# Softmax of the mix stage: exponentials taken by ScalarE from the score banks, probabilities scaled in four pieces

## What is computed

```python
scores = einsum('bcqhgd,bckhd->bchgqk', qc, kb) * HEAD_DIM ** -0.5      # 128 keys a query
scores = where(valid, scores, finfo(float32).min)
probs = softmax(concatenate([scores, sink], axis=-1), axis=-1)[..., :WINDOW]
out = einsum('bchgqk,bckhd->bcqhgd', probs, vb)
mix = concatenate([out, conv], axis=-1) @ w_o
h = layer_norm(ALPHA * h + mix)
```

## Time and profile before

| what | value |
|---|---|
| median of 3 runs | 2282.29 us (2281.48 to 2282.68) |
| span of the profiled execution, first to last instruction | 2280.0 us |
| TensorE busy (matmul) | 2111.2 us, 93% |
| VectorE busy | 1169.0 us, 51% |
| ScalarE busy | 632.4 us, 28% |
| GpSimd busy | 481.3 us, 21% |
| mean granted clock of TensorE | 0.968 of full speed |

### The profile page before, as it was taken

The page is one execution under the profiler, slowest core; times in us unless marked ns, Lnnn a source line. Parts: engine busy times, 40 slices in busy tenths (PEclk is TensorE's granted clock), DMA queues, the critical chain, the costliest instruction groups (busy, mean ns, idle before and its releaser), DMA issues. The chain is left out here.

```text
span 2280.0 us, 25840 instructions
## 1 busy us (share of the span) xinstructions
PE 2111.2 (93%) x9568; PEld 1717.9 (75%) x9568; DVE 1169.0 (51%) x1238; ACT 632.4 (28%) x912; POOL 481.3 (21%) x317
## 2 busy tenths in 40 slices
PE   4999995789889599999999999999999799999997
PEld 3788884566666378888888888888887588888886
DVE  8698983688888444434424334334344311144333
ACT  4555552344444232221121121121121300031110
POOL 5488773243443200000000000000000000002333
PEclk9999997799999799999999999999999899999999
DMA  6310125223333242112111111111210622342220
GB/s 236 138 43 35 60 74 163 64 91 108 98 100 103 96 149 74 37 37 74 37 37 58 53 37 41 70 37 37 74 37 35 224 76 87 115 134 86 76 87 37
DMA packets 125599, 185.54 MB, mean 81 GB/s; under 512 B 7361, under 2 KB 90305, under 8 KB 122305
## 3 DMA queue, kind: packets, MB, share of 16 engines
q1 hardware_dynamic: 99616, 149.31, 20.1%
q10 hardware_dynamic: 25952, 35.86, 4.4%
HBM read 117.90 MB, written 67.24 MB: 81 GB/s over the span
## 5 line engine op out<-in xcount | busy, mean ns | idle before, releaser
L1387 PE MATMUL u_mm<-u_hT_hi,u_w_hi 128*128 128x512 f32 x1408 | 549.1, 390 | 15.4 <-DVE u_hT_lo L1355 15.4
L1387 PE MATMUL u_mm<-u_hT_lo,u_w_hi 128*128 128x512 f32 x1408 | 548.8, 390 | 0.0
L1387 PE MATMUL u_mm<-u_hT_hi,u_w_lo 128*128 128x512 f32 x1408 | 548.7, 390 | 0.0
L1501 POOL TENSOR_TENSOR d_total<-d_total,d_g 128x1024 f32 x16 | 38.2, 2387 | 1406.1 <-DVE d_total L1588 1406.1
L1321 DVE TENSOR_SCALAR u_y<-u_z,u_taps,u_bias 128x2048 f32<-128x2048 f32 x43 | 57.9, 1347 | 529.9 <-ACT u_z L1269 529.9
L1387 PEld LDWEIGHTS u_mm<-u_hT_hi,u_w_hi 128*128 128x128 f32 x1408 | 265.0, 188 | 70.6 <-DVE u_hT_lo L1355 15.8
L1269 ACT COPY u_z<-u_mm 128x512 f32<-128x512 f32 x176 | 103.2, 587 | 748.8 <-PE u_mm L1387 748.8
L1387 PEld LDWEIGHTS u_mm<-u_hT_hi,u_w_lo 128*128 128x128 f32 x1408 | 265.1, 188 | 55.2
L1387 PEld LDWEIGHTS u_mm<-u_hT_lo,u_w_hi 128*128 128x128 f32 x1408 | 265.1, 188 | 55.1
L1625 PE MATMUL d_y<-d_wd_hi,d_a_hi 128*128 128x512 f32 x704 | 218.9, 392 | 20.7 <-DVE d_wd_lo L1560 20.5
L1625 PE MATMUL d_y<-d_wd_hi,d_a_lo 128*128 128x512 f32 x704 | 217.8, 390 | 0.0
(11 more groups left out here) (172 smaller groups left out, 2506.9 us busy)
## 6 DMA issues: line engine op xcount, KB each, us to landing
u_w_raw<-w_up SPq DMA_DIRECT2D x44, 512.0 KB, 5.8
d_a_raw<-gated_scr SPq DMA_DIRECT2D x32, 704.0 KB, 5.3
gated_scr<-u_y SPq DMA_DIRECT2D x21, 1024.0 KB, 4.6
d_wd_raw<-w_down SPq DMA_DIRECT2D x22, 512.0 KB, 4.7
a_xs<-x SPq DMA_DIRECT2D x16, 512.0 KB, 4.7
m_h_in<-h_scr SPq DMA_DIRECT2D x16, 512.0 KB, 3.4
h_scr<-m_r ACTq DMA_DIRECT2D x16, 512.0 KB, 4.0
h1T_scr<-m_h1T ACTq DMA_DIRECT2D x16, 512.0 KB, 4.4
```

The source lines that it names most:

```text
L1387: last = nc.tensor.matmul(mm[m][n][:], w[:, m, k, :], h[:, k, bass.ts(n, BLK)], start=(k == 0 and w is w_hi and h is hT_hi), stop=(k == KT ...
L1501: nc.gpsimd.tensor_tensor(tile_of(t), tile_of(t), g_bc[:], ALU.mult).then_inc(scaled_ok, 1)
```

## The change

The fifth part of each row of `prob`, the sink's column, goes, and with it `peak`. `soft_shift` becomes `soft_peak`: VectorE takes the maximum, then the negated peak (`fall`, the smaller of minus the scale times the maximum and minus the sink) and `rest`, sink plus `fall`. The instruction over 128x512 that wrote the shifted scores is gone. ScalarE's `exps` reads the score bank itself, in four instructions for each g of 128x128, with the scale as a constant, `fall` as bias for each partition and the sum over the keys put out to `den`; a fifth one takes the exponential of `rest` (128x4). `soft_norm` adds `rest` to `den`, takes the reciprocal, and multiplies the probabilities in four `tensor_scalar` instructions of 128x128, each with one column of `inv` for its partitions.

Each result gets a semaphore of its own. TensorE's `scores` of the next tile waits for the exponentials (`exp_ok`) instead of the shifted scores. VectorE computes `minus_sink` once at the start of the stage. To have enough semaphores, `phase_project` closes its context, and GpSimd clears its range of semaphores, so that `phase_mix` can use them.

```diff
@@ phase_project
         def sem(name):
-            return ctx.enter_context(nc.semaphore(name))
+            used.append(ctx.enter_context(nc.semaphore(name)))
+            return used[-1]
...
+        ctx.pop_all().close()
+        nums = sorted(s.num for s in used)
+        assert nums == list(range(nums[0], nums[-1] + 1))
+        nc.gpsimd.sem_clear(range(nums[0], nums[-1] + 1))
@@ phase_mix
-        prob = sb("m_prob", [P, NKV, GROUPS, KEYS + 1])
-        top, peak = sb("m_top", [P, NKV, GROUPS]), sb("m_peak", [P, NKV, GROUPS])
+        prob = sb("m_prob", [P, NKV, GROUPS, KEYS])
+        top, fall = sb("m_top", [P, NKV, GROUPS]), sb("m_fall", [P, NKV, GROUPS])
+        minus_sink, rest = sb("m_minus_sink", [P, NKV, GROUPS]), sb("m_rest", [P, NKV, GROUPS])
...
             def exps(n, g):
-                act.wait_ge(shift_ok, NKV * n.t + (g + 1))
-                nc.scalar.activation(prob[:, g, :, :], prob[:, g, :, :], ACT.Exp).then_inc(exp_ok, 1)
+                act.wait_ge(fall_ok, NKV * n.t + (g + 1))
+                after(act, probT_ps, NKV * n.t)
+                for a in range(GROUPS):
+                    nc.scalar.activation(prob[:, g, a, :], score[g][:, a, :], ACT.Exp, bias=fall[:, g, a:a + 1], scale=SCALE,
+                                         accum_out=den[:, g, a:a + 1])
+                act.wait_ge(rest_ok, NKV * n.t + (g + 1))
+                nc.scalar.activation(rest[:, g, :], rest[:, g, :], ACT.Exp).then_inc(exp_ok, 1)
...
+            nc.vector.tensor_scalar(minus_sink[:, :, :], sink[:, :, :], -1.0, None, ALU.mult).then_inc(msink_ok, 1)
+            dve.wait_ge(msink_ok, 1)
...
-            def soft_shift(n, g):
-                dve.wait_ge(score_ps, NKV * n.t + (g + 1))
+            def soft_peak(n, g):
+                at = NKV * n.t + (g + 1)
+                dve.wait_ge(score_ps, at)
...
-                nc.vector.tensor_reduce(top[:, g, :], score[g][:, :, :], AX.X, ALU.max).then_inc(soft_seq, 1)
-                dve.wait_ge(soft_seq, soft_at(n, g, 1))
-                nc.vector.scalar_tensor_tensor(out=peak[:, g, :], in0=top[:, g, :], scalar=SCALE, in1=sink[:, g, :], op0=ALU.mult,
-                                               op1=ALU.max).then_inc(soft_seq, 1)
-                dve.wait_ge(soft_seq, soft_at(n, g, 2))
-                after(dve, probT_ps, NKV * n.t)
-                nc.vector.tensor_tensor(prob[:, g, :, KEYS], sink[:, g, :], peak[:, g, :], ALU.subtract).then_inc(soft_seq, 1)
-                nc.vector.scalar_tensor_tensor(out=prob[:, g, :, 0:KEYS], in0=score[g][:, :, :], scalar=SCALE,
-                                               in1=along(peak[:, g, :], KEYS), op0=ALU.mult, op1=ALU.subtract).then_inc(shift_ok, 1)
+                nc.vector.tensor_reduce(top[:, g, :], score[g][:, :, :], AX.X, ALU.max).then_inc(top_ok, 1)
+                dve.wait_ge(top_ok, at)
+                after(dve, exp_ok, NKV * n.t - 1 + g)
+                nc.vector.scalar_tensor_tensor(out=fall[:, g, :], in0=top[:, g, :], scalar=-SCALE, in1=minus_sink[:, g, :],
+                                               op0=ALU.mult, op1=ALU.min).then_inc(fall_ok, 1)
+                dve.wait_ge(fall_ok, at)
+                after(dve, den_ok, NKV * n.t - 1 + g)
+                nc.vector.tensor_tensor(rest[:, g, :], sink[:, g, :], fall[:, g, :], ALU.add).then_inc(rest_ok, 1)

             def soft_norm(n, g):
-                dve.wait_ge(exp_ok, NKV * n.t + (g + 1))
-                nc.vector.tensor_reduce(den[:, g, :], prob[:, g, :, :], AX.X, ALU.add).then_inc(soft_seq, 1)
...
-                nc.vector.reciprocal(inv[:, g, :], den[:, g, :]).then_inc(soft_seq, 1)
...
-                nc.vector.tensor_tensor(prob[:, g, :, 0:KEYS], prob[:, g, :, 0:KEYS], along(inv[:, g, :], KEYS), ALU.mult).then_inc(prob_ok, 1)
+                at = NKV * n.t + (g + 1)
+                dve.wait_ge(exp_ok, at)
+                nc.vector.tensor_tensor(den[:, g, :], den[:, g, :], rest[:, g, :], ALU.add).then_inc(den_ok, 1)
+                dve.wait_ge(den_ok, at)
+                nc.vector.reciprocal(inv[:, g, :], den[:, g, :]).then_inc(inv_ok, 1)
+                dve.wait_ge(inv_ok, at)
+                for a in range(GROUPS):
+                    v = nc.vector.tensor_scalar(prob[:, g, a, :], prob[:, g, a, :], inv[:, g, a:a + 1], None, ALU.mult)
+                v.then_inc(prob_ok, 1)
...
@@ scores of TensorE
-                after(pe, shift_ok, NKV * n.t)
+                after(pe, exp_ok, NKV * n.t)
```

More of the change, by code:

```diff
@@ L122, in sb @@
             return ctx.enter_context(nc.sbuf_tensor(name, shape, dt))
+        used = []
         def sem(name):
-            return ctx.enter_context(nc.semaphore(name))
+            used.append(ctx.enter_context(nc.semaphore(name)))
+            return used[-1]
         hT_hi = sb("a_hT_hi", [P, KT, SEQ], F32R)
@@ L676, in phase_mix @@
         conv_hi_ok, conv_lo_ok, attn_hi_ok, attn_lo_ok = (sem("m_" + n) for n in ("conv_hi", "conv_lo", "attn_hi", "attn_lo"))
-        vw_ok, shift_ok, exp_ok, prob_ok, probT_ok = (sem("m_" + n) for n in ("vw", "shift", "exp", "prob", "probT"))
+        vw_ok, exp_ok, prob_ok, probT_ok = (sem("m_" + n) for n in ("vw", "exp", "prob", "probT"))
+        msink_ok, top_ok, fall_ok, rest_ok, den_ok, inv_ok = (sem("m_" + n) for n in ("msink", "top_ok", "fall_ok", "rest_ok", "den_ok", "inv_ok"))
         resid_ok, lv_ok, ly_ok, norm_ok, scaled_ok, h1_ok, h1T_ok = (sem("m_" + n) for n in ("resid", "lv", "ly", "norm", "scaled", "h1", "h1T"))
-        soft_seq, cn_seq, ln_seq, z_seq, lact_seq, cact_seq, stats_seen = (sem("m_" + n) for n in ("soft_seq", "cn_seq", "ln_seq", "z_seq", "lact_seq", "cact_seq", "stats_seen"))
+        cn_seq, ln_seq, z_seq, lact_seq, cact_seq, stats_seen = (sem("m_" + n) for n in ("cn_seq", "ln_seq", "z_seq", "lact_seq", "cact_seq", "stats_seen"))
         block = ctx.enter_context(nc.Block())
@@ L978, in row_norm @@
                 assert seq.n == 6
-            def soft_at(n, g, k):
-                return n.t * (NKV * 5) + (3 * g + k)
-            def soft_shift(n, g):
-                dve.wait_ge(score_ps, NKV * n.t + (g + 1))
+            def soft_peak(n, g):
+                at = NKV * n.t + (g + 1)
+                dve.wait_ge(score_ps, at)
                 if isinstance(n.t, int) and n.t == 0:
@@ L994, in soft_shift @@
-                nc.vector.tensor_tensor(prob[:, g, :, KEYS], sink[:, g, :], peak[:, g, :], ALU.subtract).then_inc(soft_seq, 1)
-                nc.vector.scalar_tensor_tensor(out=prob[:, g, :, 0:KEYS], in0=score[g][:, :, :], scalar=SCALE,
-                                               in1=along(peak[:, g, :], KEYS), op0=ALU.mult, op1=ALU.subtract).then_inc(shift_ok, 1)
-            def soft_norm(n, g):
-                dve.wait_ge(exp_ok, NKV * n.t + (g + 1))
-                nc.vector.tensor_reduce(den[:, g, :], prob[:, g, :, :], AX.X, ALU.add).then_inc(soft_seq, 1)
-                dve.wait_ge(soft_seq, n.t * (NKV * 5) + (3 * NKV + 2 * g + 1))
-                nc.vector.reciprocal(inv[:, g, :], den[:, g, :]).then_inc(soft_seq, 1)
-                dve.wait_ge(soft_seq, n.t * (NKV * 5) + (3 * NKV + 2 * g + 2))
-                nc.vector.tensor_tensor(prob[:, g, :, 0:KEYS], prob[:, g, :, 0:KEYS], along(inv[:, g, :], KEYS), ALU.mult).then_inc(prob_ok, 1)
+                nc.vector.tensor_reduce(top[:, g, :], score[g][:, :, :], AX.X, ALU.max).then_inc(top_ok, 1)
@@ L1044, in step @@
                     log_gate(c)
-                soft_shift(n, 0)
+                soft_peak(n, 0)
                 if c is not None:
                     swish(c)
-                soft_shift(n, 1)
+                soft_peak(n, 1)
                 if c is not None:
```

## The result

The changed kernel takes 2296.93 us (median of 4 runs, 2294.34 to 2298.28), the kernel before in the same comparison 2282.07 (4 runs, 2281.48 to 2282.68): a ratio of 1.0063 [1.0049, 1.0077]. It is slower by 14.9 us.

What follows compares the result with a forecast made beforehand. The step was taken as a loop through TensorE and VectorE's softmax chain, held by GpSimd; 20.8 + 7.7 + 0.2 = 28.7 us on a span of 2280.0 gave 2308.7, 2311 as median, range 2297 to 2327.

Steps and rivals of the forecast that it cites:

- The pieces wait for GpSimd: In soft_norm, tensor_scalar pieces stand still until the running GpSimd instruction ends; g = 0 is held, g = 1 runs free.
- The signs that the prediction named: Around 560: first addition about 2.2 us, a g = 0 piece 1.5 to 2.3, g = 1 pieces 0.3, TensorE idle before g = 0.
- steps of 24.7 us: Sign in the mix stage: each full step would last 24.7 us if the forecast was right.
- faster: Rival: pieces with a column operand don't wait for GpSimd, only the additions do; 2260 to 2272 us, chance 0.11.
- no difference: Rival: pieces wait, but those of g = 0 all get through between two GpSimd instructions; 2277 to 2282 us, chance 0.06.
- 13 steps x 1.6 = 20.8: Mix stage: the scaling of g = 1 ends 1.6 us later in each of 13 steps, 20.8 us in all.
- the lower bound of 1.3: Least delay a step, if pieces follow each other without any handing over and GpSimd's last short instruction is short.
- the prediction's clock: Time scale of the profiled step of the kernel before whose softmax starts at 560.11, used for all forecast event times.
- 5 x 1.53 = 7.7: TensorE's clock: all 13 steps become the slow kind, five of them losing 1.53 us each; bounds 0 and 20.
- I put 0, with 1 us either way: First two tiles of the mix: passes saved are worth at most what they take; put at 0, 1 us either way.
- Terms of 0 that held: ScalarE's exponentials ready before VectorE wants them, and GpSimd's semaphore clearing covered before its fills: each put at 0.
- the edges with minus_sink: First and last tiles put at 0; minus_sink at the stage start put at 0.2 us, up to 2.

Runs made afterwards that it cites:

- Experiment 3: The changed kernel without GpSimd's gain and bias instructions of the norm after the mix (two over 128x1024 a step): 2217.92 us, 0.9717 of the kernel before.
- experiment 8: The changed kernel with ScalarE's exponentials left in the score bank in PSUM, where the four scaling pieces read them: 2264.07 us, 0.9925 of the kernel before.
- experiment 1: The kernel before with only the scaling of the probabilities split into four tensor_scalar pieces, nothing of ScalarE's part: 2330.71 us, 1.0213 of the kernel before.
- experiment 2: The changed kernel with the scaling put back into one multiplication for each g, ScalarE's exponentials kept: 2297.77 us, 1.0065 of the kernel before.
- experiment 6: The changed kernel with one scaling multiplication for each g, and softmax and conv norm operands in PSUM so neither waits for GpSimd: 2226.78 us, 0.9761 of before.
- 4: The kernel before with only the softmax reciprocals moved from SBUF to a dead corner of the score bank in PSUM: 2252.11 us, 0.9867 of the kernel before.
- 5: The changed kernel with one scaling multiplication for each g, and reciprocals and the exponential of rest in PSUM: 2235.93 us, 0.9805 of the kernel before.
- 7: The kernel before with reciprocals and conv norm in PSUM and exps(n, 1) ahead of conv_root, nothing of the change: 2234.88 us, 0.9797 of the kernel before.

## Why the prediction was right in its mechanism and wrong in its size

**The pieces wait for GpSimd** (right). The signs that the prediction named are in the rows of the result, but for steps of 24.7 us, which are 23.99: the addition of 2.26 ending with L792, a piece of 2.27 ending 0.09 behind L794, the pieces of g = 1 free, L993 1.09 us earlier from L1002 (3.88 against 4.97), the idle time ahead of g = 0. Experiment 3 takes GpSimd's two instructions away and the loss with them, experiment 8 lets the pieces alone go free and ends faster than before. The rivals "faster" and "no difference" fall by the same rows: a piece that meets L794 does not last 0.3, and the pieces do not all get through between two GpSimd instructions.

The Trainium skill (SBUF — State Buffer, Who interferes with whom) says that tensor_scalar can take the pair of ports, and that tensor_reduce never contends. By that rule, the trace agrees: 2.27 us for a piece, and 0.68 for the sum L1000 of experiment 1 beside a running L783.

**"13 steps x 1.6 = 20.8"** (failed in size). From the first maximum to the second transposes it is 12.85 us, before 11.63: 1.22 more a step, 15.9 in all. That is below even the lower bound of 1.3. Laid over the prediction's clock (5.87 less than the rows above):

| event | forecast | measured |
|---|---|---|
| L993 starts | 563.88 | 563.99 |
| L792 ends | 567.17 | 567.29 |
| L794 ends | 569.66 | 569.74 |
| L778 ends | 571.3 | 571.23 |
| fourth piece of g = 0 ends | 571.9 | 571.71 |
| fourth piece of g = 1 ends | 573.3 | 572.90 |

Up to L778 the sum holds within 0.12. The third piece, put at 571.6, ends at 571.51. The fourth was put a whole length of 0.3 behind it and follows after 0.20. The last group was put at 1.4, where its own terms (0.2 + 0.2 + 0.92) make 1.32; it took 1.19, because the addition starts 0.08 before the row ahead of it ends and the pieces take 0.87. A chain of short instructions has to be summed from start to start.

**"5 x 1.53 = 7.7", the clock** (failed in size, the pattern right). All 13 steps have a clock of 0.93 now, as forecast. But here the low clock costs less than it did. The windows of the low clock, after

```profile
577.60:581.30 3.70, 3.42 (x12) 2.76 (x13) 2.86 (x11) 1.17 (x2) 0.00 (x0) 0.54 0.00 0
```

and in the kernel before

```profile
571.70:577.20 5.50, 5.46 (x26) 3.79 (x27) 4.17 (x7) 1.38 (x3) 1.63 (x2) 0.69 0.00 0
```

hold the same time at 1.2 GHz, half of full speed: 3.70 x 0.46 x 2 and 5.50 x 0.31 x 2 are both 3.4 us. Now it starts with the transposes of g = 0 (0.95 instead of 0.63), behind which TensorE waits for VectorE anyway (0.16). That may be why it costs less; no run isolates it. From the second transposes to the next scores it is 9.91 in this step, where it was 10.31 in a step of the slow kind and 8.78 in one at full clock: 1.13 is lost, not 1.53. 13 x 1.13 against 8 x 1.53 is 14.7 against 12.2, so 2.5 us were added, not 7.7. With 15.9 that makes 18.4 of the 18.8 measured; the rest lies in steps a little unlike this one, as 24.28 in the first window shows.

**The edges, "I put 0, with 1 us either way"** (failed). The first two tiles gained 2.2 us and the tail 1.0. Of the 2.2, 1.2 lie in the last step ahead of the full ones: it takes 19.05 us (426.26 to 445.31), before 20.27 (427.23 to 447.50). It takes 19.0 to 19.1 in all six kernels with ScalarE's part, with pieces or without, and 20.2 to 20.3 in the four without it. So the saved passes do count there, and the pieces cost nothing. The other 1.0 lies further ahead, where the kernels with ScalarE's part differ by more than that, and not by whether they have pieces (the changed kernel reaches this step at 426.26; of those without pieces experiment 2 at 424.21 and experiment 6 at 427.46). It was not traced further, nor were the 1.0 of the tail and the 0.8 in later stages.

**Terms of 0 that held.** ScalarE was never late: g = 0 is ready at 569.93 and wanted at 570.92, g = 1 at 572.03 and wanted at 577.50. The clearing of semaphores makes GpSimd's first fill 0.3 us later than SyncE's first load (370.29 and 370.00, before 369.77 and 369.78), covered as argued.

Together: 15.9 + 2.5 - 3.2 + 0.8 = 16.0 on the span, and with the 0.5 of unlike steps 16.5, where 28.7 was forecast. Of the 12.7 between 16.0 and 28.7 the clock is 5.2, the chain 4.9, and the edges with minus_sink and the later stages 2.6.

## What to carry to other kernels

Before splitting or adding a VectorE instruction beside a busy GpSimd, look at whether it can be made to wait. In these runs that was a tensor_scalar with source and result in SBUF, or an instruction with two tensor operands there; each can be left behind a whole GpSimd instruction whatever its size. An addition over 128x4 cost 2.26 us here, and the waits of the pieces 33 us of the kernel's time. The remedy is to let one operand come from PSUM, in a corner that is dead at that time: two lines gave 31 us, all such edits 47 in the kernel before and 55 with ScalarE's part. What a pass taken off an engine is worth depends on the waits behind it: ScalarE's part was a loss of 15 us while the softmax waited (experiment 2), a gain of 15 once it no longer did (4 against 5), and of 8 with no waits left (7 against 6).

## What the runs showed that was not expected

- Waiting depends on the operation and on where its operands lie, not on its size. Beside a running GpSimd instruction, with source and result in SBUF, a sum over 128x516 took 0.68 and a reciprocal 0.18 (experiment 1), as if alone; a tensor_scalar over 128x128 did wait; the same with its source in PSUM did not, four in 1.12 (experiment 8). An instruction with two tensor operands waited with both in SBUF (2.26) and not with one in PSUM (0.15).
- At a change of hands the waiting VectorE instruction comes first and GpSimd's next right behind it, so that as a rule one VectorE instruction gets through for each of GpSimd's. In experiment 1 a second piece slipped through, in the 0.08 us between two rows of GpSimd that are joined by a semaphore (586.40 and 586.48); between L794 and L778, whose rows overlap, none did.
- ScalarE's output of sums is a row of its own, in the list of lines between 450 and 765 us (busy us, mean ns, idle before):

```profile
L837 ACT ACTIVATE m_prob<-m_score,m_fall 128x128 f32<-128x128 f32 x108 | 38.1, 364 | 0.0
L837 ACT ACTIVATION_READ_ACCUMULATOR m_prob<-m_score,m_fall 128x1 f32 x108 | 21.9, 203 | 0.0
```

  With it an exponential over 128x128 is followed by the next after 0.35 us (568.33 to 569.72 for four).
- A stretch at the low clock costs a different amount by where in the step it lies. 3.4 us at 1.2 GHz cost 1.13 us in the changed kernel and 1.53 in the kernel before. Longer stretches cost more: 5.2 us (6.90 x 0.38 x 2) cost 2.2 in experiment 1 (565.6 to 572.5).
